# Normalising the attention probabilities on VectorE before they are transposed, in place of spreading their inverses with products

## What is computed

```python
s = einsum(q, k) * ATTN_SCALE - slope * distance      # masked where the pattern has no key
m = max(s, -1);  p = exp(s - m);  den = sum(p, -1)
o = einsum(p, v) / den                                 # per pattern; the three are mixed
w = softmax(stack(lses));  attn = sum(w * stack(outs)) # by their log-denominators

def _mem_attention(q, km, vm):
    s = einsum('nlhd,nmhd->nhlm', q, km) * ATTN_SCALE
    p = softmax(s, axis=-1)
    return einsum('nhlm,nmhd->nlhd', p, vm)
```

## Time and profile before

| | us |
|---|---|
| median of 3 runs | 1087.69 |
| lowest and highest | 1084.55, 1089.52 |
| the profiled execution | 1084.03 |
| its span in the trace | 1082.2 |
| attention stage in the trace | about 213 to 461 |

### The profile page before, as it was taken

How to read it: one execution, slowest core, us unless ns; L and a number is a source line. 1 busy time by engine, 2 the same in 40 slices (tenths; PEclk the granted TensorE clock), 3 DMA queues, 4 the chain that set the end, 5 groups by cost and what they waited for, 6 DMA issues and landing times.

```text
span 1082.2 us, 16454 instructions
## 1 busy us (share of the span) xinstructions
PE 970.9 (90%) x6540; PEld 748.2 (69%) x6540; DVE 346.7 (32%) x743; ACT 272.6 (25%) x580; POOL 151.1 (14%) x242
## 2 busy tenths in 40 slices
PE   6999999968989998799997379999999999999575
PEld 6999889834655555478885368778878878877331
DVE  5202110176546555835444800010001001001056
ACT  5202110034334444812222011111111111111054
POOL 0000000422112212400000012112112211211000
PEclk9999999999999999989998579999999999999787
DMA  9999996599667566096215939999899999991354
GB/s 333 328 365 320 377 333 257 216 274 312 247 244 246 176 216 208 13 337 233 78 64 178 332 101 326 302 316 319 298 297 317 321 311 327 325 322 38 136 213 150
DMA packets 116281, 273.42 MB, mean 253 GB/s; under 512 B 13984, under 2 KB 82080, under 8 KB 113408
## 3 DMA queue, kind: packets, MB, share of 16 engines
q1 hardware_dynamic: 107456, 247.97, 66.8%
q0 software_dynamic: 8768, 24.66, 6.5%
HBM read 256.33 MB, written 95.30 MB: 325 GB/s over the span
## 4 chain that ended last, share of the span: by engine, by line
PE 81%; DVE 8%; issue 4%; DMA 3%; ACT 3%; POOL 1%; SPq 0%; DVEq 0%; POOLq 0%; ACTq 0%
PE psum L642 76%; PE psum L701 4%; DMA back<-pair_d 1%; DVE front L1476 1%; ACT front L1092 1%; POOL back L1611 1%; DVE back L1208 1%; PE psum L845 1%; DMA middle<-pair_d 0%; DVE middle L1240 0%; DVE middle L1562 0%; DMA back<-h_d,back 0%; DMA back<-w_in 0%; DVE middle L1241 0%; DMA pair_d<-front,back 0%
## 5 line engine op out<-in xcount | busy, mean ns | idle before, releaser
L642 PE MATMUL psum<-back,front 128*64 128x128 f32 (+2 forms) x1280 | 149.9, 302 | 11.5 <-DVE back L490 7.9
L642 PEld LDWEIGHTS psum<-back,front 128*64 128x64 f32 (+2 forms) x1280 | 108.8, 164 | 45.9 <-issue 30.8
L642 PE MATMUL psum<-front 64*128 64x512 f32 (+5 forms) x448 | 120.5, 506 | 12.1 <-DVE stats L1208 7.4
L642 PE MATMUL psum<-back 128*128 128x112 f32 (+3 forms) x1152 | 123.1, 307 | 2.2 <-issue 2.0
L642 PEld LDWEIGHTS psum<-back 128*128 128x128 f32 (+1 forms) x1152 | 111.8, 170 | 14.5 <-issue 8.8
L642 PE MATMUL psum<-back,middle 128*128 128x112 f32 (+1 forms) x880 | 101.8, 316 | 1.7 <-issue 1.7
L642 PE MATMUL psum<-x_high,w_high 128*128 128x352 f32 x288 | 94.1, 327 | 8.3 <-DVE w_low L358 8.3
L642 PEld LDWEIGHTS psum<-back,middle 128*128 128x128 f32 (+1 forms) x880 | 91.3, 181 | 14.5 <-issue 14.5
L642 PEld LDWEIGHTS psum<-front 64*128 64x128 f32 (+2 forms) x448 | 51.5, 191 | 66.1 <-issue 48.3
L642 PE MATMUL psum<-x_low,w_high 128*128 128x352 f32 x288 | 93.4, 324 | 0.0
L642 PE MATMUL psum<-x_high,w_low 128*128 128x352 f32 x288 | 93.2, 324 | 0.0
(11 more groups left out here) (186 smaller groups left out, 1237.7 us busy)
## 6 DMA issues: line engine op xcount, KB each, us to landing
out_win_k_s<-cache_win_k SPq DMA_DIRECT2D x16, 2044.0 KB, 13.9
out_win_v_s<-cache_win_v SPq DMA_DIRECT2D x16, 2044.0 KB, 13.4
front<-w_down SPq DMA_DIRECT2D x16, 1024.0 KB, 7.6
middle<-w_gate SPq DMA_DIRECT2D x16, 1024.0 KB, 6.6
back<-w_up SPq DMA_DIRECT2D x16, 1024.0 KB, 8.6
back<-winkT SPq DMA_DIRECT2D x8, 1792.0 KB, 7.9
back<-cache_win_v SPq DMA_DIRECT2D x8, 1024.0 KB, 6.7
front<-w_gate SPq DMA_DIRECT2D x8, 1024.0 KB
```

The costliest lines, as they stand in the source:

```text
L642: return nc.tensor.matmul(out, lhsT, rhs, start=start, stop=stop, skip_group_check=True)
```

## The change

VectorE now normalises the probabilities in place, in SBUF, before they are transposed. The new helper `divided(u, s)` waits for the exponential of head s, inverts its one denominator and multiplies the 128 x w probabilities with it (w = 128(i+1), or 256). It is called for unit u+1 from unit u: head 0 at item 1, head 1 at item 3, or at the last item where there are fewer; for unit 0 ahead of the loop. The transposes of a unit wait for it (`s_norm`) and no longer for the exponential. The spreading products, the GpSimd loop, `spread` and `inverse` are gone, and `o_out` is now one ScalarE copy from PSUM to `CAT`, in the place of `spread`. Mins, exponentials, transposes, values and extra steps are the same and in the same order.

```diff
@@ pe: transposes, values
-                    pe.wait_ge(s_exp, 2 * u + 2)
+                    pe.wait_ge(s_norm, 2 * u + 2)
...
-                if blocks[-1] == nb - 1:
-                    pe.wait_ge(s_dg, u + 1)
-                    for s in range(2):
-                        last = mm(b[64 * s:64 * s + 64, P:2 * P], ones[:, 0:HD], DG[u % 2][:, s, :], True, True)
-                    last.then_inc(s_O, 1)
@@ act
-            def spread(u):
-
-                act.wait_ge(s_O, u + 1)
-                if u:
-                    act.wait_ge(s_OB, u)
-                nc.scalar.copy(INV, bank(6 + u % 2)[:, P:2 * P]).then_inc(s_inv, 1)
+            def o_out(u):
+                kind, hp, i = units[u]
+                act.wait_ge(s_PV, unit_items[u][-1] + 1)
+                if (kind, hp, i) in (("w", 2, 0), ("c", 0, 0)):
+                    act.wait_ge(s_xp, xnum[("pool", 4) if kind == "w" else ("pv", 1, 3)] + 1)
+                nc.scalar.copy(CAT[:, hp + (0 if kind == "w" else 6), i * P:i * P + P], bank(6 + u % 2)[:, 0:P]).then_inc(s_OB, 1)
...
-                        spread(u - 1)
+                        o_out(u - 1)
@@ dve
-            def inverse(u):
-
-                dve.wait_ge(s_exp, 2 * u + 2)
-                V_.reciprocal(RD[:, 2 * u:2 * u + 2], DEN[:, 2 * u:2 * u + 2]).then_inc(s_rd, 1)
-
-            def o_out(u):
+            def divided(u, s):
                 kind, hp, i = units[u]
...
+                w = P * (i + 1) if kind == "w" else N_MEM
+                x = 2 * u + s
+                p = SP[(u % 3) * 2 + s][:, 0:w]
+                dve.wait_ge(s_exp, x + 1)
+                V_.reciprocal(RD[:, x:x + 1], DEN[:, x:x + 1]).then_inc(s_rd, 1)
+                dve.wait_ge(s_rd, x + 1)
+                V_.tensor_scalar(p, p, RD[:, x:x + 1], None, ALU.mult).then_inc(s_norm, 1)
...
+            for s in range(2):
+                divided(0, s)
...
-                    if j == 0:
-                        inverse(u)
                     for s in range(2):
                         if u + 2 < NU and j == min(2 * s, len(mine) - 1):
                             mins(u + 2, s)
-                        if u and j == s == 0:
-                            o_out(u - 1)
+                    for s in range(2):
+                        if u + 1 < NU and j == min(2 * s + 1, len(mine) - 1):
+                            divided(u + 1, s)
@@ pool
-            for u in range(NU):
-                pool.wait_ge(s_rd, u + 1)
-                if u >= 2:
-                    pool.wait_ge(s_O, u - 1)
-                for s in range(2):
-                    last = G.tensor_scalar(DG[u % 2][:, s, :], ident, RD[:, 2 * u + s:2 * u + s + 1], None, ALU.mult)
-                last.then_inc(s_dg, 1)
```

More of the change, by code:

```diff
@@ L183, in build @@
         SBIAS = at(49808, 960)
-        DG = [at(50768 + 2 * P * s, 2, P) for s in range(2)]
         KN = at(51280, 512)
-        INV = at(51792, P)
         OA = at(51280, 512)
@@ L245, in build @@
         s_S, s_min, s_exp = sem("s_S"), sem("s_min"), sem("s_exp")
-        s_rd, s_dg, s_inv = sem("s_rd"), sem("s_dg"), sem("s_inv")
-        s_T, s_Td, s_Ta, s_PV, s_O, s_OB = sem("s_T"), sem("s_Td"), sem("s_Ta"), sem("s_PV"), sem("s_O"), sem("s_OB")
+        s_rd, s_norm = sem("s_rd"), sem("s_norm")
+        s_T, s_Td, s_Ta, s_PV, s_OB = sem("s_T"), sem("s_Td"), sem("s_Ta"), sem("s_PV"), sem("s_OB")
         s_xp, s_xe, s_sexp, s_smin, s_srd = sem("s_xp"), sem("s_xe"), sem("s_sexp"), sem("s_smin"), sem("s_srd")
@@ L1038, in _ @@
                     nc.scalar.copy(high, full).then_inc(s_hi, 1)
-            spread(NU - 1)
+            o_out(NU - 1)
             def cat_rounded(c):
@@ L1216, in evac @@
                     transposed_out(dve, V_.tensor_copy, n).then_inc(s_Td, 1)
-            def inverse(u):
-                dve.wait_ge(s_exp, 2 * u + 2)
-                V_.reciprocal(RD[:, 2 * u:2 * u + 2], DEN[:, 2 * u:2 * u + 2]).then_inc(s_rd, 1)
-            def o_out(u):
+            def divided(u, s):
                 kind, hp, i = units[u]
-                dve.wait_ge(s_inv, u + 1)
-                if (kind, hp, i) in (("w", 2, 0), ("c", 0, 0)):
-                    dve.wait_ge(s_xp, xnum[("pool", 4) if kind == "w" else ("pv", 1, 3)] + 1)
-                b = bank(6 + u % 2)
-                V_.tensor_tensor(CAT[:, hp + (0 if kind == "w" else 6), i * P:i * P + P], b[:, 0:P], INV,
-                                 ALU.mult).then_inc(s_OB, 1)
+                w = P * (i + 1) if kind == "w" else N_MEM
[5 more added lines that the diff above has]
+                V_.tensor_scalar(p, p, RD[:, x:x + 1], None, ALU.mult).then_inc(s_norm, 1)
             def normalised(c):
@@ L1345, in _ @@
                     V_.tensor_tensor(low, full, high.bitcast(F32), ALU.subtract).then_inc(s_lo, 1)
-            o_out(NU - 1)
             def cat_rest(c):
```

## The result

The kernel after takes 1076.61 us in the median of 14 runs (1070.68 to 1081.41), the kernel before 1084.35 in 14 (1076.52 to 1089.52): a ratio of 0.9919, 95% interval 0.9899 to 0.9939, so 0.8% faster (8.8 us by the ratio, 7.7 by the medians). Two later comparisons gave 0.9919 (0.9896 to 0.9941) and 0.9902 (0.9878 to 0.9926). The forecast was 2 us faster in a range of 1077 to 1097: too small a gain, by 6 to 7 us. Its median, 1085.7, was laid on the three runs of before known then (1087.69, where 14 runs give 1084.35), so 3.3 of the 9.1 us between it and 1076.61 belong to that base and not to the change. The profiled execution of after took 1078.85 us, with a span of 1076.4.

The account below looks back on a forecast made before the run. TensorE was taken to pace units 6 to 39, VectorE the first units, VectorE and ScalarE the split; 1.3 - 6.0 + 2.7 = -2.0 us gave 1082.0 profiled, 1085.7 as median, range 1077 to 1097.

Parts of the forecast that it names:

- Price of the new work: VectorE's multiplications cost 0.353 us at 256 columns, 0.75 at 1024; net it gets about 42 us of work.
- Units 0 to 5: Start of the attention stage, VectorE the later engine: the added divisions make unit 6 1.3 us late (0 to 3).
- against the profiled execution (1084.03): The final sum: 1.3 - 6.0 + 2.7 = -2.0 us, taken from before's profiled execution, giving 1082.0.
- Units 6 to 31: Middle of the stage, TensorE sets the pace: without spreading products and their waits it gains 6.0 us.
- The rival that the division hides: VectorE's late starts cost nothing in units 0 to 39, only the split pays: -5.8 to -7.6 us, 1080; chance 0.20.
- the rival of stuck evacuations: Wide units (i = 4 to 7): evacuations wait behind multiplications, 0.75 us in each of 16; 1099, at half 1091; chance 0.15.
- Units 32 to 39: Memory units: VectorE's division enters the loop, 2.32 us a unit; +0.3 without extra step, steps start earlier; +0.7 in all.
- Units 40 to 47: Memory units beside the weight split: VectorE is the bound, 3.15 us a unit instead of 2.38; 5.2 us lost.
- The tail: From unit 47's transposes to CAT's first rest: 7.24 us before, then +4.0 without the GpSimd hops; 3.2 us back.
- The clock rival: TensorE's waits bring the lower clock in units 32 to 39, +0.9 us for each of 8 units: 1093; chance 0.10.
- its own range: The forecast case's range, 1082 to 1091: 0 to 3 in units 0 to 5, gain 4 to 7, 0 to +5 in the rest.
- The rest of the kernel follows `mix` ... I take it as moved by the whole shift: Everything behind the stage, from `mix` on, moves by the stage's whole shift, -2.0 us.

Follow-up runs that it names:

- before_filler: The kernel before with idle identity products on TensorE in the last four units and ahead of the output projection; projection 116.58 us instead of 119.2.
- the padding: Semaphore increments nobody waits for, ahead of the combination: 48 on ScalarE in before, 0.9969 and 0.9956 of before; 45 in after, 0.9947 and 0.9978 of before.

## Why the prediction was wrong, step by step

- **Price of the new work: right.** 96 multiplications took 44.6 us, 464 ns each, and 96 reciprocals 15.1; VectorE's busy time rose by 35 us, against "some 42".
- **Units 0 to 5: right for the trace that it was worked from, wrong for the kernel.** +1.2 to +1.5 at full clock, -0.7 where the clock falls, which is the usual case in before. The step that failed is the sum made "against the profiled execution (1084.03)": that execution's entry was the one in five at 2.4 GHz, and with it any relief of an entry at half clock could not be seen. It costs 1.9 us of the difference.
- **Units 6 to 31: near in size, with luck in it.** 6.0 forecast, 6.1 in the first pair of traces, 6.5 in the means (unit 8 to unit 32). But in that pair the clock's fall in unit 14 took 1.2 us more from after than from before. Unit 14 left out, the gain is 7.3 us: 3.2 in the one-item units with an extra step (2.8 forecast), 2.2 in those with two items (2.2), and the wide units with i = 5 and 6, put at nothing, gave 0.22 or 0.07 each.
- **The rival that the division hides: right in these units, wrong in the others.** It costs 0.05 us a unit in 17 to 31, which also refutes the rival of stuck evacuations (0.75 a unit). But the division costs 3.6 us up to unit 8 and 4.1 in units 32 to 39, where that rival had put nothing.
- **Units 32 to 39: right in sum (+1.1, forecast 0.7), by two misses that cancel.** The plain pair of units 38 and 39 came out at 2.43 us each, forecast 2.32. But units 33 and 37, put at +0.3 each, lost 0.95 and 1.06, because VectorE's work for an extra step stands ahead of the division there. The four units with a step, put at -0.5 together (0.7 less 4 x 0.3), gained 1.7. That the sum is right is luck.
- **Units 40 to 47: nearly** (+4.4, forecast 5.2), with VectorE the bound. **The tail: nearly** (-2.7, forecast -3.2).
- **The clock rival: wrong about the place, and small.** PEclk was 1.00 from 404.8 to 432.9, where the rival had looked. Against the change the clock fell more often in unit 14 (0.7 us in the means) and in the tail. The tail took 6.04 us where it fell and 5.1 where it did not; in before it took 8.6 at either clock. In favour of the change it counted at the entry and at the start of `mix`.
- **Two sums of the prediction do not add up**, without effect on the forecast: its own range reaches down to 1080.7 (0 - 7 + 0 = -7), not 1082, and half of the stuck evacuations gives 1092, not 1091.
- **"The rest of the kernel follows `mix` ... I take it as moved by the whole shift": this step failed.** 5.0 us lie behind the first product of `mix`: 1.1 in the projection's first products at half clock (shown by before_filler), 0.7 between the projection and the combination (in the means; its cause is open), and 3.2 in the combination. For these the padding shows that pieces of program which the change moved are a cause; how much of the 3.2 is theirs it does not settle, since a late load also lets TensorE's clock fall (0.76 over the combination in before, 0.80 in after) and the sixth and seventh load scatter by themselves.

## What to carry to other kernels

Walk the stage instruction by instruction, as here, but check each part against the trace and not only the sum: here the stage came out within half a microsecond though two units of it lost 1 us each that nobody had put down, and others made up for it. Where a new wait turns an engine's output into the pacing engine's input, charge everything else that stands ahead of it on that engine. Then ask the same of what lies behind it: how long TensorE idles before the next stretch and at which clock that one begins. Look at more than one trace before a term is taken from a stretch with short waits: a stage entry at 1.2 GHz and one at 2.4 differ by 4 us here, more than the whole forecast. An edit that changes the number of instructions moves the places where program is loaded; a difference of 3 us in a distant stage that streams data may be nothing else, and a few idle increments on that engine tell.

## What the runs showed of the hardware

- A load of 1 MB that took 5.7 to 6.2 us landed in 7.1 to 8.8 us in eight of the ten cases in which a piece of program (0.01 to 0.02 MB) was loaded while it was under way.
- TensorE's clock could be held at 2.4 GHz through waits of 1 to 4 us by idle products of the identity (0.39 us a product of `mix` from the second on, instead of 0.77 and 0.63).
- A VectorE multiplication in SBUF (128x256, 0.35 us) stood 2.25 us while GpSimd combined two SBUF operands; a reciprocal of one column beside it was not held up.
- 120 and 130 semaphore increments in a row kept TensorE for 17.24 and 18.78 us, 0.14 us each. Where it would have waited 13.94 us anyway, they lengthened the stretch by 1.3 and 2.8 us.
- The same stretch of the same kernel ran at either clock from execution to execution: from the transposes of unit 14 to those of 15, 9.24 us at full clock and 10.6 to 12.0 where it fell behind a wait of 2.2 to 2.4 us.
